# Differential sums of the last two units in other PSUM banks, and the raw gate copied out by ScalarE

## What is computed

```
proj = h @ w_in
rq, rk, rv, rg, dq, dk, dv = jnp.split(proj, points, axis=-1)
...
o = (o_f + o_b).astype(f32)                        # retention, 8 heads, both directions
mu = jnp.mean(o, axis=-1, keepdims=True)
var = jnp.mean(jnp.square(o - mu), axis=-1, keepdims=True)
o = (o - mu) * lax.rsqrt(var + EPS)
ret_out = (jax.nn.silu(rg.astype(f32)) * o).astype(h.dtype)
...
p = jax.nn.softmax(s, axis=-1)                     # differential attention, 8 heads
a = p[:, :, 0] - lam * p[:, :, 1]
od = jnp.einsum("bhqk,bhkv->bhqv", a, vd)
od = od * lax.rsqrt(jnp.mean(od * od, axis=-1, keepdims=True) + EPS) * diff_subln_w * (1.0 - lam_init)
...
return jnp.concatenate([ret_out, diff_out], axis=-1) @ w_out
```

## Time and profile before

| | us |
|---|---|
| three runs, median | 3374.86 (3372.33 to 3378.23) |
| profiled execution, own time | 3374.02 |
| its span | 3372.2 |
| PE busy in the span | 3269.3 |
| VectorE busy | 2772.4 |
| ScalarE busy | 1057.7 |
| GpSimd busy | 1152.3 |
| heads, from the first stall of PE in them to the last | 268 to 811 |

### The profile page before, as it was taken

How to read it: one execution, slowest core, us unless ns; L and a number is a source line. 1 busy time by engine, 2 the same in 40 slices (tenths; PEclk the granted TensorE clock), 3 DMA queues, 4 the chain that set the end, 5 groups by cost and what they waited for, 6 DMA issues and landing times.

```text
span 3372.2 us, 48323 instructions
## 1 busy us (share of the span) xinstructions
PE 3269.3 (97%) x19317; PEld 2995.0 (89%) x19317; DVE 2772.4 (82%) x3941; ACT 1057.7 (31%) x1414; POOL 1152.3 (34%) x575
## 2 busy tenths in 40 slices
PE   7999999999997999999999999999999999999998
PEld 2688888888996447999999999999999999999997
DVE  5888888888877558987888888888788888888887
ACT  2322323232323002872323233323322323332322
POOL 2443333333350468002333333233123333333331
PEclk9999999999998999999999999999999999999999
DMA  9644444444646411469989999999899999999996
GB/s 403 246 166 160 162 162 158 165 155 141 248 176 250 137 63 51 182 236 343 357 351 360 357 354 363 348 351 356 306 357 353 358 346 355 356 353 349 355 347 238
DMA packets 173325, 916.65 MB, mean 272 GB/s; under 512 B 16176, under 2 KB 53977, under 8 KB 79961
## 3 DMA queue, kind: packets, MB, share of 16 engines
q1 hardware_dynamic: 123894, 555.47, 44.4%
q0 software_dynamic: 49248, 358.63, 27.3%
HBM read 878.41 MB, written 34.55 MB: 271 GB/s over the span
## 4 chain that ended last, share of the span: by engine, by line
PE 79%; DVE 12%; DMA 4%; issue 4%; ACT 1%; POOL 0%; SPq 0%; DVEq 0%; ACTq 0%
PE ps_all L1045 17%; PE ps_all L1107 9%; PE ps_all L1106 9%; PE ps_all L1112 9%; PE ps_all L1052 9%; PE ps_all L1010 6%; PE ps_all L741 5%; PE ps_all L743 5%; PE ps_all L742 5%; DMA sb_raw_ring<-in_v_t 2%; DVE sb_hot L2004 2%; DVE sb_tops L1724 1%; DVE sb_hot L2001 1%; PE ps_all L687 1%; DMA sb_col_ring_w<-in_ada_wt 1%
## 5 line engine op out<-in xcount | busy, mean ns | idle before, releaser
L1407 ACT ACTIVATE sb_raw_hi<-sb_raw_ring 128x2048 fp32r<-128x2048 f32 x256 | 491.0, 1918 | 1146.8 <-DMA sb_raw_ring<-in_v_t 581.8
L1920 DVE TENSOR_TENSOR sb_raw_lo<-sb_raw_ring,sb_raw_hi 128x2048 fp32r<-128x2048 f32 x256 | 585.5, 2287 | 108.8 <-ACT sb_raw_hi L1407 108.4
L1106 PE MATMUL ps_all<-sb_w_hi,sb_raw_hi 128*128 128x342 f32 x2048 | 645.5, 320 | 12.3 <-issue 5.2
L1045 PE MATMUL ps_all<-sb_h_hi,sb_raw_hi 128*128 128x342 f32 x2048 | 646.0, 320 | 0.0
L1045 PE MATMUL ps_all<-sb_h_lo,sb_raw_hi 128*128 128x342 f32 x2048 | 645.7, 320 | 0.0
L1107 PE MATMUL ps_all<-sb_w_lo,sb_raw_hi 128*128 128x342 f32 x2048 | 644.8, 321 | 0.0
L2224 POOL DMA_INDIRECT sb_gather_ring<-in_u_tab,sb_kept x171 | 288.8, 1689 | 757.5 <-DVE sb_kept L2050 580.5
L2224 POOL DMA_INDIRECT sb_gather_ring<-in_v_tab,sb_kept x171 | 303.7, 1776 | 620.2 <-DVE sb_acc_a L2063 406.7
L2154 POOL TENSOR_TENSOR sb_w_low<-sb_w_raw,sb_w_high 128x2048 fp32r<-128x2048 f32 (+1 forms) x64 | 267.5, 4179 | 427.9 <-ACT sb_w_high L1223 427.9
L1106 PEld LDWEIGHTS ps_all<-sb_w_hi,sb_raw_hi 128*128 128x128 f32 x2048 | 389.0, 190 | 14.4 <-issue 8.5
L1107 PEld LDWEIGHTS ps_all<-sb_w_lo,sb_raw_hi 128*128 128x128 f32 x2048 | 387.6, 189 | 0.0
(11 more groups left out here) (297 smaller groups left out, 5472.9 us busy)
## 6 DMA issues: line engine op xcount, KB each, us to landing
sb_raw_ring<-in_u_t SPq DMA_DIRECT2D x128, 1024.0 KB, 6.9
sb_raw_ring<-in_v_t SPq DMA_DIRECT2D x128, 1024.0 KB, 7.5
sb_arena<-in_ada_wt SPq DMA_DIRECT2D x96, 512.0 KB, 4.3
sb_w_raw<-in_w_t SPq DMA_DIRECT2D x32, 1024.0 KB, 4.9
sb_w_raw<-in_w_v SPq DMA_DIRECT2D x32, 768.0 KB, 4.3
sb_g_ring<-table_scratch SPq DMA_DIRECT2D x32, 684.0 KB, 10.5
sb_arena<-in_ada_w SPq DMA_DIRECT2D x10, 2048.0 KB, 12.4
table_scratch<-sb_stage SPq DMA_DIRECT2D x8, 2432.0 KB, 8.0
```

Of the source, the lines that this page charges most:

```text
L1045: last = mm(acc, raw_hi[:, r[0], kk * P:(kk + 1) * P], part[:, kk, :], start=i == 0, stop=False)
L1106: mm(accs[c], v, w_hi[:, slots[e], :], start=e == 0, stop=False)
L1407: acti(raw_hi[:, k % 2, :], raw_ring[:, k % RAW, :], ACT.Copy).then_inc(S["un_hi"], 1)
L1920: vec.tensor_tensor(raw_lo[:, k % RAW, :], raw_ring[:, k % RAW, :], raw_hi[:, k % 2, :].bitcast(f32), ALU.subtract)\
```

## The change

Three things are changed, all within the heads:

1. The differential sums of units 2 and 3 are made in banks 4 and 5 (`dif_sum(u)`), where the scores and then the transposes of the same units stood. `dif_values` of units 2 and 3 no longer waits for `dif_n`. In return `out_transposes(a, 0)`, which writes bank 4, waits for `dif_n` of unit 2.
2. The raw gate gets a place in SBUF between the two values (`vg`), and ScalarE copies all 384 columns of a tile out in one instruction. VectorE's multiplication then reads that copy and writes the gate over it. ScalarE's copy waits for `ret_n` of the head before, since `ret_norm` reads the old gate.
3. `p(0)` to `p(3)` of the next head wait for ScalarE's `proj_ev` of their bank and no more for VectorE's `gate`. So does the first transpose of the last head.

```diff
--- before.py
+++ after.py
@@ -187,9 +187,9 @@
 
         take = carver(small)
         k_t, q_t, dk_t, dq_t = (take(T) for _ in range(4))
-        vd = take(NT * 2 * P).rearrange("p (t m c) -> p t m c", t=NT, m=2)
+        vg = take(NT * 3 * P).rearrange("p (t m c) -> p t m c", t=NT, m=3)
+        vd, gate = vg[:, :, 0:3:2, :], vg[:, :, 1, :]
         e_g = take(NT * P).rearrange("p (t c) -> p t c", t=NT)
-        gate = take(NT * P).rearrange("p (t c) -> p t c", t=NT)
         dist = take(2 * 384).rearrange("p (s u) -> p s u", s=2)
         decay_log = take(384)
         decay_tab = take(384)
@@ -378,6 +378,9 @@
         def y_turned(t):
             return psum[:, 4 * NB * (1 - t % 2):4 * NB * (2 - t % 2)]
 
+        def dif_sum(u):
+            return bank(6 + u if u < 2 else 2 + u)[:, 0:P]
+
         def groups_of(unit):
             return unit // TPG, unit % TPG
 
@@ -764,7 +767,7 @@
                 r = n % 2
                 if n < 4:
 
-                    wait(pe, "gate", 4 * (h - 1) + n + 1)
+                    wait(pe, "proj_ev", 8 * (h - 1) + 5 + n)
                     for k in range(KD):
                         c = slice(k * P, (k + 1) * P)
                         last = split_products(bank(n), ((w_high[:, r, c], w_low[:, r, c]), (h_hi[:, k, :], h_lo[:, k, :])),
@@ -802,7 +805,7 @@
                 g, m = groups_of(u)
                 wait(pe, "proj_ev", 8 * a + 4)
                 if u < 2:
-                    wait(pe, "dif_n", 4 * (a - 1) + u + 3)
+                    wait(pe, "dif_n", 4 * (a - 1) + u + 1)
                 else:
                     wait(pe, "ret_pd", 2 * a + u - 1)
                 b = bank(6 + u if u < 2 else 2 + u)
@@ -836,19 +839,17 @@
                 wait(pe, "dif_te", 4 * a + u + 1)
                 if u < 2:
                     wait(pe, "ret_n", a + 1)
-                else:
-                    wait(pe, "dif_n", 4 * a + u - 1)
                 for s in range(TPG):
-                    last = mm(bank(6 + u % 2)[:, 0:P], attn_t[:, u, s, :], vd[:, g * TPG + s, 1, :],
+                    last = mm(dif_sum(u), attn_t[:, u, s, :], vd[:, g * TPG + s, 1, :],
                               start=s == 0, stop=s == TPG - 1)
                 last.then_inc(S["dif_v"], 1)
 
-            def out_transposes(a, w):
+            def out_transposes(a, w, last_head=False):
                 wait(pe, "dif_te", 4 * a + 3 + w)
                 if w == 0:
                     wait(pe, "ret_n", a + 1)
-                else:
-                    wait(pe, "dif_n", 4 * a + 4)
+                if w or not last_head:
+                    wait(pe, "dif_n", 4 * a + 3 + w)
                 src = diff_o if w else ret_o
                 for t in range(NT):
                     last = nc.tensor.transpose(bank(4 + w)[:, t * P:(t + 1) * P], src[:, t, :], ident[:, :])
@@ -944,7 +945,7 @@
             for u in range(2):
                 dif_scores(a, u)
 
-            pe.wait_ge(S["gate"], NT * HEADS)
+            pe.wait_ge(S["proj_ev"], 8 * HEADS)
             pe.wait_ge(S["late_cols"], 1)
             pe.wait_ge(S["bias_in"], 80)
             nc.tensor.transpose(bank(0)[0:GROUPS * LATE, 0:P], late_all[:, 0:GROUPS * LATE], ident[:, :]).then_inc(S["late_t"], 1)
@@ -961,11 +962,11 @@
             pe.wait_ge(S["mix_hi"], 1)
             for t in range(NT):
                 wo_high_part(t, range(HEADS - 1))
-            out_transposes(a, 0)
+            out_transposes(a, 0, last_head=True)
             pe.wait_ge(S["mix_lo"], 1)
             for t in range(NT):
                 wo_low_part(t, range(HEADS - 1))
-            out_transposes(a, 1)
+            out_transposes(a, 1, last_head=True)
             pe.wait_ge(S["mix_lo"], 2)
             for t in range(NT):
                 last = wo_part(t, 0, 0, (HEADS - 1,))
@@ -1244,8 +1245,9 @@
                     wait(act, "ret_v", 2 * (h - 1) + g + 1)
                     wait(act, "dif_v", 4 * (h - 1) + 2 * g + 2)
                     wait(act, "gate", 4 * (h - 1) + t + 1)
+                    wait(act, "ret_n", h)
                     v = bank(t)[:, 0:3 * P].rearrange("p (m c) -> p m c", m=3)
-                    acti(vd[:, t, :, :], v[:, 0:3:2, :], ACT.Copy)
+                    acti(vg[:, t, :, :], v, ACT.Copy)
                     acti(e_g[:, t, :], v[:, 1, :], ACT.Exp, scale=-1.0).then_inc(S["proj_ev"], 1)
 
             def soft_exp(a, u):
@@ -1263,7 +1265,7 @@
 
             def dif_square(a, u):
                 wait(act, "dif_v", 4 * a + u + 1)
-                acti(soft[:, u, 0, 0:P], bank(6 + u % 2)[:, 0:P], ACT.Square, accum_out=dif_ss[:, u:u + 1])\
+                acti(soft[:, u, 0, 0:P], dif_sum(u), ACT.Square, accum_out=dif_ss[:, u:u + 1])\
                     .then_inc(S["dif_sq"], 1)
 
             def out_evacuate(a, w):
@@ -1698,8 +1700,7 @@
                     last = vec.tensor_scalar(ret_o[:, t, :], sums[t], mv[:, t, 0:1],
                                              nt_y[:, 4 + t:5 + t], ALU.subtract, ALU.mult)
                 link(last)
-                vec.scalar_tensor_tensor(ret_o.rearrange("p t c -> p (t c)"), ret_o.rearrange("p t c -> p (t c)"), 1.0,
-                                         gate.rearrange("p t c -> p (t c)"), ALU.mult, ALU.mult).then_inc(S["ret_n"], 1)
+                vec.scalar_tensor_tensor(ret_o, ret_o, 1.0, gate, ALU.mult, ALU.mult).then_inc(S["ret_n"], 1)
 
             def dif_norm(a, pair, link):
                 wait(dve, "dif_sq", 4 * a + 2 * pair + 2)
@@ -1707,14 +1708,14 @@
                 link(vec.tensor_scalar(nt_a[:, 0:2], dif_ss[:, 2 * pair:2 * pair + 2], 1.0 / P, EPS, ALU.mult, ALU.add))
                 rsqrt(link, nt_y[:, 4:6], nt_a[:, 0:2], nt_y[:, 0:2], nt_b[:, 0:2])
                 for j in range(2):
-                    vec.tensor_scalar(diff_o[:, 2 * pair + j, :], bank(6 + j)[:, 0:P], nt_y[:, 4 + j:5 + j], None, ALU.mult)\
+                    vec.tensor_scalar(diff_o[:, 2 * pair + j, :], dif_sum(2 * pair + j), nt_y[:, 4 + j:5 + j], None, ALU.mult)\
                         .then_inc(S["dif_n"], 1)
 
             def silu_gate(h, t, link):
                 wait(dve, "proj_ev", 8 * h + 5 + t)
                 link(vec.scalar_tensor_tensor(e_g[:, t, :], e_g[:, t, :], 1.0, e_g[:, t, :], ALU.add, ALU.max))
                 link(vec.reciprocal(e_g[:, t, :], e_g[:, t, :]))
-                vec.tensor_tensor(gate[:, t, :], e_g[:, t, :], bank(t)[:, P:2 * P], ALU.mult).then_inc(S["gate"], 1)
+                vec.tensor_tensor(gate[:, t, :], e_g[:, t, :], gate[:, t, :], ALU.mult).then_inc(S["gate"], 1)
 
             def late_piece(n, w, silu, place, part, used):
                 half, c = n % 2, n // 2
```

## The result

| | us |
|---|---|
| kernel before, median of the comparison | 3376.45 (3372.33 to 3378.23) |
| changed kernel, median | 3351.2 (3347.97 to 3353.16) |
| ratio | 0.993, 95% interval 0.9918 to 0.9942 |
| profiled execution of the changed kernel, own time and span | 3349.33 and 3347.5 |

A forecast was written before the change was run, and what follows sets the result against it. PE, busy for 97% of the span, was taken as the bound. The terms 16.4 + 6.2 + 0.4 - 0.1 - 1.7 = 21.2 us, off 3374.0, gave 3352.8, stated as 3353, range 3347 to 3361.

The forecast's parts named there:

- The wait for `dif_n`: Before `dif_values` of units 2 and 3: PE's stall goes in seven turns, 7 x 2.35 = 16.4 us gained.
- The low clock behind it: Block behind the `dif_values` stall: PE keeps full clock after four of seven stalls, 4 x 1.55 = 6.2 us gained.
- The first rival: Behind `dif_values`: the clock falls all the same, only the stalls go, some 16 us gained, 3358 us; chance 12%.
- The wait for `gate` at `p(0)`: Start of the next head's projections: PE's 0.14 us wait for VectorE goes in three turns, 0.4 us gained.
- The longer copy: ScalarE's copy of 384 columns takes 0.1 us more per tile; uncovered only before the last head, 0.1 us lost.
- The multiplication, cost 0: VectorE's L1717 reading both inputs from SBUF: no longer itself, any hold by GpSimd covered in the turns, 0 us.
- the second rival: In the turns: VectorE becomes the bound through holds by GpSimd, leaving a gain of 8 us, 3366 us; chance 9%.
- The moved wait: Wait for `dif_n` now in `out_transposes`: 7.6 us of cover, so it costs 0.
- The way into the last head: Before the last head: VectorE gains 2.2 us where PE gains 3.9, so 1.7 us are lost.
- The sign that I had named: In the last head: PE's wait at the transposes grows by 1 to 2 us.
- Everything behind moves up as a whole: Stages behind the heads: they start when their inputs are there and move up as a whole; no term of their own.
- The stall only moves: Behind L842: PE's next wait, L2154 for `p(6)` or `p(7)`, takes the stall up; no change, 3374 us; chance 4%.

The follow-up runs named there:

- e5: The changed kernel run again, unaltered, against the kernel before: median 3350.9 us against 3373.2, ratio 0.9928.
- e3: Kernel before with only the gate copied out and `p(0)` waiting for `proj_ev`; sums stay in banks 6 and 7: median 3372.4 us, ratio 0.9997.
- e1: Kernel before with 12 unused matmuls put before the wait for `dif_n`, which stays: median 3368.4 us, ratio 0.9984.
- e2: Kernel before with only the sums of units 2 and 3 moved to banks 4 and 5: median 3371.1 us, ratio 0.9997.
- e4: Changed kernel, but `p(0)` to `p(3)` wait for VectorE's `gate` again: median 3368.7 us, ratio to the kernel before 0.9991.
- e7: Changed kernel with three more VectorE instructions of 1024 columns behind the gates of each turn: median 3389.6 us, ratio to the kernel before 1.0054.

## Why the prediction was right

It forecast 3353 us and 21.2 us less for the profiled execution; measured were 3351.2 and 24.7. In the turns, where the change works, the forecast holds best: 23.0 us (16.4 + 6.2 + 0.4) against 23.7 measured from the first stall to the last out transposes, and 23.7 again in e5. How near the totals come is in part luck: the profiled execution of e5 is 17.8 us shorter than that of before, with the same heads. By its steps:

*The wait for `dif_n`, 16.4 us.* Right in place and size. The distance to `dif_values` is 0.17 us in all seven turns; before, it was 2.50 to 2.55. The seven differences sum to 16.5. e3 has the stall without it.

*The low clock behind it, 6.2 us.* Right, and shown by e1: no fall of the clock in the turns once PE has work, whatever it is. The first rival, a clock that falls there for another reason, is out. (The 0.9 that it takes off in its sum has no row behind it; by the working for the last head it would be 0.15, for PE would be 2.35 us sooner there and VectorE can be 2.2.)

*The wait for `gate` at `p(0)`, 0.4 us.* The short periods went from 89.7 to 87.2, 2.55 us where the stall alone gives 2.35, so it was 0.2 in each of three turns. The side remark that some 2 us of each stall would come back without the third part is the true weight of this step: e2 and e4 show 2.4 us in each of six turns, and the clock's falls as well. Counted on its own the step is worth 0.4 us in the turns (e3, 0.9 less what lies ahead of them), as forecast, but the first part is worth only 3.4 without it.

*The longer copy.* ScalarE's L1250 takes 0.49 us, 0.11 more than before (forecast 0.1). The 0.1 us lost before the last head can't be told apart.

*The multiplication, cost 0.* Right for PE, and the hold that was feared is real: 3.99 to 4.13 us in each of six turns. The page "SBUF — State Buffer" of the Trainium skill says in "Who interferes with whom" that two inputs in SBUF contend with GpSimd's reads; the trace agrees, for L1717 with one input in PSUM took 0.29 us in all 32 cases, four of which began while GpSimd's L2154 ran. In e2, which has it so, the multiplication of tile 1 started at the same place, behind the start of GpSimd's instruction, and took 0.29 us as well, and its neighbour with two inputs in SBUF took 3.92:

```profile
559.72 0.29 DVE L1718 TENSOR_TENSOR sb_small<-sb_small,ps_all 128x128 f32<-128x128 f32 x1
559.93 3.92 DVE L1716 SCALAR_TENSOR_TENSOR sb_small<-sb_small 128x128 f32<-128x128 f32 x1
...
559.10 4.60 POOL L2155 TENSOR_TENSOR sb_w_low<-sb_w_raw,sb_w_high 128x2048 fp32r<-128x2048 f32 x1 [5.85 <-ACT sb_w_high L1224]
```

So the hold mostly changed its victim, as the second rival's counter-argument had it. It was closer than its chance of 9% says, though: of 6.3 us of waits 2.1 are left, since 2.35 went with the shorter turn and VectorE is busy for 1.9 us more, and e7 shows what is behind them. That rival's way of adding the lateness up gives too little: in e7 a late VectorE met a further hold.

*The moved wait, cost 0.* Right: PE's wait at L855 is the 0.30 us of before.

*The way into the last head, 1.7 us lost.* The size was right (1.8: VectorE 22.55 us ahead, PE 24.3). The sign that I had named was wrong. I expected PE's wait at the transposes to grow by 1 to 2 us; it shrank by 1.7, as the matmuls ahead of it took 1.7 us longer at the low clock. The loss itself is VectorE's, as the step has it, and PE meets it sooner, up to the new wait at L813.

*Everything behind moves up as a whole.* Most of the 3.5 us between forecast and result come from outside the turns: 0.6 before them, 1.7 from the fall of the clock behind the start of the queries, 1.2 elsewhere between the last head and the table building, and 0.7 lost again from there to the end. The turns gave 0.7 more than forecast. The range allowed for the fall as "one or two falls"; as it comes and goes between executions with no tie to the change, these 1.7 us are chance.

*The stall only moves.* This rival had 4% for the full change. It is what happens to the first part alone (e2), though at `p(0)` and not at the weights of `p(6)` or `p(7)`, where the prediction looked for it. With the other parts alone (e3) the stall stays where it was.

## What to carry to other kernels

Before a stall is taken away, look for the next instruction of the same engine that waits for the same helper: here the two waits, 2.35 us at one place and 0.14 at another, hid one behind the other, and each part of the cure alone measured as nothing. A short stall of PE has a second price in its clock, to be read from the granted clock of the block behind it. And count what is left of the helper's waits afterwards: here VectorE had 2.1 us of waits in a turn, and 3.7 us of added work in each of six turns, 22 in all, cost 31.

## What was not expected of the hardware

- Equal stalls did not have equal effects on the clock. The stalls of `dif_values` were followed by 1.2 GHz in four of seven cases both in the kernel before (the first, third, fifth and seventh) and in e3 (the first, second, fifth and seventh), and those at `p(0)` in three of six (e2) and four of six (e4). What decides between them no run here shows.
- 3.7 us more work on VectorE in a turn (e7) cost up to 10.4 us in that turn (97.57 against 87.18) and nothing in the next.
- The pass over the tables behind the heads took 1877.4 us in one profiled execution (the kernel before) and 1887.6 in another (e1), with the same instructions in it. The runs of the kernel before spread from 3366.7 to 3379.9 us (31 runs), and up to 3385.3 in ten more. A gain of 2 us must be read from the trace.
